# Expert weights loaded in transfers of one, two and four chunks in a float32 two-model kernel

## The chip, the core and the metric

The kernel runs on one core of one Trainium2 chip. The metric is the device time of one execution in microseconds (us); lower is better.

## The reference

One token sequence of 256 rows and 1024 features, all in float32, goes through two small models one after the other. The first has two layers. Each is a mixer (convolutions in layer 0, a gated linear recurrence in layer 1), a layer norm, and a mixture of experts: 16 experts, each with three matrices of 1024 x 1024, and every token goes to two of them. The second model has a layer of forgetting attention, a layer of dilated attention, and a convolutional feed-forward block behind each.

```
def moe(x, w_router, b_router, w1, w3, w2):
    e_idx, gates = route(xf, w_router, b_router)      # top 2 of 16
...
    def expert_block(args):
        xb, e = args
        hb = jax.nn.silu(xb @ w1[e]) * (xb @ w3[e])
        return hb @ w2[e]
```

## The kernel before

**Chunks.** All weights are read once from HBM, in the order in which they are used, in chunks of 128 partitions x 2048 float32 values: 8 KB a partition, 1 MB in all. `STREAM` (L39) lists them: 14 chunks of the first mixer, 192 of layer 0's experts (`moe0`), 14 of the second mixer, 192 of `moe1`, then those of the second model. An expert has twelve chunks: four of w1, four of w3, four of w2. Below, a chunk of a layer is named by its number 0 to 191 in `moe0` or `moe1`; expert 10 has 120 to 131.

**Places.** The chunks go to 24 places of 8 KB a partition: twelve in the tensor `ring` (places 0 to 11), five in `F` (12 to 16), four in `early` (17 to 20), and one each in `Z` (21), `XT` (22) and at another spot of `F` (23, used once a layer). Each place has its own semaphore. In the second model only seven ring places are used. `_place_stream` (L124) fixes at build time which chunk goes where. The first 24 positions of an expert layer are written out by hand (`FIRST_SLOTS`), because the places come free one by one when the mixer and the routing are done; chunk 3 is moved back to position 17 of its layer. After them each chunk takes the place whose last chunk is the oldest. Places outside the ring and Z are given out only up to position 127 of a layer, since other work needs them later. So 23 places rotate up to position 127 and 13 after it. The tables `SLOT`, `PREVIOUS` (the chunk that lay there before) and `LOADS` (how many loads a place has had) come from this.

**Loading.** `sync_load` (L327) runs on SP. For each chunk it waits until the previous chunk of its place was released, and then issues one transfer that counts on the place's semaphore. SP does this strictly in the order of the chunks, in stretches: up to chunk 119 of a layer, up to 155, and then on. The last chunk of a layer is loaded in two halves, each 4 KB a partition (L338, L339). Everything goes to one hardware queue, SP's.

**Use.** `tensor_product` (L1096) waits for a chunk with `landed` and runs it through TensorE (L1112): up to 64 tokens of the expert as the stationary operand, one pass of 512 columns of weights at a time, on the two halves of the array's columns. The profile shows eight matmul records a chunk. After its last matmul the chunk's release is signalled. Between w3 and w2 of an expert TensorE also turns the hidden values, and on alternate experts gathers the next pair's tokens (L1092) or adds the results back to the tokens (L1166). Dense weights (all but the experts') are first split into a high and a low part by ScalarE and VectorE (L360, L366) and then multiplied (L383 to L385).

**In HBM** a chunk of an expert matrix lies in one piece, its rows of 8 KB one behind the other: the array is [layer, expert, 4, 128, 2048], built by `layout`. There is also a path for experts with more than 64 tokens (`overflow_sync`, L1608), behind a branch at expert 12; it reads the same arrays.

Of the kernel before, what the change touches and what calls it, by code (L numbers as in the profile page):

```python
# [15 lines left out]
T, D, NT, KD = 256, 1024, 2, 8  # L16
# [3 lines left out]
RING, SMALL_RING, EXTRA = 12, 7, 12  # L20
PIECE, NPIECE = 512, 4
PE_TAPS = 11
CH = 2048
# [95 lines left out]
LOAD_ORDER = list(range(len(KIND)))  # L119

LAST_CHUNKS = (CHUNK["moe0"] + 191, CHUNK["moe1"] + 191)


def _place_stream():  # L124
    for layer in range(2):
        m, at = CHUNK[f"moe{layer}"], FIRST_SLOTS[layer].index(ONCE_SLOT)
        LOAD_ORDER[m + 3:m + at + 1] = LOAD_ORDER[m + 4:m + at + 1] + [m + 3]
    last, loads = [None] * (RING + EXTRA), [0] * (RING + EXTRA)
    SLOT.extend([None] * len(KIND))
    PREVIOUS.extend([None] * len(KIND))  # L130
    LOADS.extend([None] * len(KIND))
    for position, n in enumerate(LOAD_ORDER):
        slots = [*range(RING), Z_SLOT] if n < CHUNK["aq0"] else list(range(SMALL_RING))
        slot = None
        if KIND[n] == "expert":
            layer = int(n >= CHUNK["moe1"])
            i = position - CHUNK[f"moe{layer}"]
            if i < len(FIRST_SLOTS[layer]):
                slot = FIRST_SLOTS[layer][i]
            elif i < 128:  # L140
                slots += [*F_SLOTS, *SPLIT_SLOTS, XT_SLOT]
        if slot is None:
            slot = min(slots, key=lambda x: -1 if last[x] is None else last[x])
        SLOT[n], PREVIOUS[n] = slot, last[slot]
        last[slot] = n
        loads[slot] += n > 0
        LOADS[n] = loads[slot]

# [41 lines left out]
class Kernel:  # L190
    def __init__(self, nc, ctx, A, out, known):
# [9 lines left out]
        def dma_sem(name):  # L201
# [17 lines left out]
        self.X = sb("X", [128, NT, D])  # L219
        self.Z = sb("Z", [128, NT, D])  # L220
        self.XT = sb("XT", [128, KD, T])
        f_at = (nc.sbuf_base + 31) // 32 * 32
# [31 lines left out]

        self.slots = [self.ring[:, i, :] for i in range(RING)] + [
            self.F[:, 12672 - 2048 * i:14720 - 2048 * i] for i in range(5)] + [self.early[:, i, :] for i in range(4)] + [
            self.Z[:, :, :].rearrange("p h d -> p (h d)"), self.XT[:, :, :].rearrange("p k t -> p (k t)"),
            self.F[:, 2304:4352]]
        self.over = [dma_sem(f"s_over_{n}") for n in ("pe", "act", "dve", "w")]
# [18 lines left out]
    def source(self, n):  # L278
        A = self.A
# [11 lines left out]
        if name.startswith("moe"):  # L291
            return A[("w1", "w3", "w2")[i // 4 % 3]][int(name[3]), i // 12, i % 4]
        return tensors[name][order[name][i] if name in order else i]

    def chunk(self, n):
        return self.slots[SLOT[n]]

    def landed(self, n):
        return self.ring_sems[SLOT[n]], 16 * LOADS[n]

# [26 lines left out]
    def sync_load(self, first, last):  # L327
        sp = self.sp
        for n in LOAD_ORDER[first:last]:
            if n == CHUNK["aq0"] + 3:  # L330
                self.sync_rows()
            if KIND[n] == "expert" and SLOT[n] >= RING:
                sp.wait_ge(*self.extra_free(n))
            if PREVIOUS[n] is not None:
                sp.wait_ge(self.released(PREVIOUS[n]))
            src = self.source(n)
            if n in LAST_CHUNKS:
                sp.e.dma_start(self.chunk(n)[:, 0:1024], src[:, 0:1024]).then_inc(self.s_last, 16)  # L338
                sp.e.dma_start(self.chunk(n)[:, 1024:2048], src[:, 1024:2048]).then_inc(self.ring_sems[SLOT[n]], 16)  # L339
            else:  # L340
                sp.e.dma_start(self.chunk(n)[:, 0:src.shape[-1]], src).then_inc(self.ring_sems[SLOT[n]], 16)

# [1265 lines left out]
    def overflow_sync(self, layer, expert):  # L1608
        s_pe, _, _, s_w = self.over
        e, wb = self.nc.sync, self.overflow_views()["wb"]  # L1610
        for w in range(3):
            for c in range(4):
                if w + c:
                    e.wait_ge(s_pe, 4 * w + c + (1 if w == 2 else 0))
                e.dma_start(wb, self.A[("w1", "w3", "w2")[w]][layer, expert, c].rearrange("a p n -> (a p) n")
                            ).then_inc(s_w, 16)

# [851 lines left out]
    def dilated_views(self):  # L2469
        F = self.F  # L2470
        XF = self.XT[:, :, :].rearrange("p k t -> p (k t)")
        ZF = self.Z[:, :, :].rearrange("p h d -> p (h d)")
        spare = self.ring[:, 7:10, :].rearrange("p r c -> p (r c)")
# [388 lines left out]
def layout(i):  # L2862
# [34 lines left out]
    for k, n in (("w1", "moe_w1"), ("w3", "moe_w3"), ("w2", "moe_w2")):  # L2897
        w = i[n]
        a[k] = c(w.reshape(2, 16, 4, 2, 128, 1024).transpose(0, 1, 2, 4, 3, 5).reshape(2, 16, 4, 128, 2048))
    by_columns = i["moe_w2"][:, 15].reshape(2, 2, 4, 128, 2, 512).transpose(0, 4, 1, 3, 2, 5).reshape(2, 4, 128, 2048)  # L2900
    a["w2"] = c(np.concatenate([a["w2"][:, :15], by_columns[:, None]], axis=1))
# [37 lines left out]
```

## Time and profile before

| | |
|---|---|
| three runs, us | 1788.22, 1788.83, 1787.92; median 1788.22 |
| span of the profiled execution, us | 1787.6 |
| TensorE busy, share of the span | 96% |
| VectorE, ScalarE, GpSimd busy | 44%, 35%, 7% |
| read from HBM | 542.19 MB, 304 GB/s over the span |
| granted TensorE clock, mean | 0.998 |

The profiled execution has no time of its own beside its span; the span is 0.6 us below the median. The page divides the span into 40 slices of 44.7 us, and a digit is the busy share of a slice in tenths. Times in the rows below are microseconds from the start of the span unless ns is written. A busy TensorE is not a TensorE at its peak. In the rows SPq is SP's sequencer, PE is TensorE, PEld its weight loads, DVE VectorE, ACT ScalarE.

### The profile page before, as it was taken

To read this page: it belongs to the slowest core of one execution; us is meant where nothing else is said; L and a number is where in the kernel's file an instruction comes from. 1 tells how busy PE (TensorE), PEld (TensorE's weight loads), DVE (VectorE), ACT (ScalarE), POOL (GpSimd) and SP (SyncE) were. 2 spreads that over 40 slices of the span, in tenths; PEclk is the share of its full clock that TensorE was granted. 3 is DMA by queue.
4 is the path that set the end of the run, shared out by engine and by line. 5 is a ranking of instruction groups with operands and counts; after the bars stand their busy time and mean duration, and the time that the engine had idled before them with its cause. 6 is when DMAs were issued, how large, how long until landed. Compare 5 with 4: busy or idle time off the path is not lost.

```text
span 1787.6 us, 24011 instructions
## 1 busy us (share of the span) xinstructions
PE 1720.1 (96%) x10024; PEld 1114.5 (62%) x10024; DVE 790.6 (44%) x1510; ACT 624.1 (35%) x1197; POOL 121.0 (7%) x143
## 2 busy tenths in 40 slices
PE   9999999999899989999999989999999999999998
PEld 8974344433234974444333333887999899789986
DVE  6961111111003782111111011866888677768875
ACT  5541110000002661000000001666666564656664
POOL 0000000000000000000000000131111001401100
PEclk9999999999999999999999999999999999999999
DMA  9569999999999779999999999543555544435550
GB/s 390 236 249 409 423 424 423 422 422 421 419 421 419 279 298 391 423 423 424 422 422 421 419 420 420 194 141 120 188 189 177 199 159 150 141 120 179 186 189 24
DMA packets 76100, 544.91 MB, mean 305 GB/s; under 512 B 8528, under 2 KB 8528, under 8 KB 10576
## 3 DMA queue, kind: packets, MB, share of 16 engines
q1 hardware_dynamic: 75600, 542.15, 75.9%
q8 instruction: 83, 1.36, 0.3%
q10 hardware_dynamic: 384, 1.13, 0.2%
q14 instruction: 33, 0.27, 0.0%
HBM read 542.19 MB, written 1.05 MB: 304 GB/s over the span
## 4 chain that ended last, share of the span: by engine, by line
PE 71%; DMA 17%; DVE 7%; ACT 3%; issue 1%; POOL 1%; SPq 0%; DVEq 0%; ACTq 0%
PE PS L1112 25%; DMA ring<-in_w 17%; PE PS L383 12%; PE PS L385 11%; PE PS L384 11%; PE PS L1092 2%; PE PS L1166 2%; DVE wl L366 2%; PE PS L834 1%; PE PS L593 1%; ACT wh L360 1%; PE PS L1128 1%; PE PS L1180 1%; PE PS L1275 0%; DVE F L969 0%
## 5 line engine op out<-in xcount | busy, mean ns | idle before, releaser
L1112 PE MATMUL PS<-ring,F 128*64 128x512 f32 x1992 | 454.4, 597 | 30.4 <-DMA ring<-in_w 22.8
L366 DVE TENSOR_TENSOR wl<-ring,wh 128x512 fp32r<-128x512 f32 x504 | 363.6, 740 | 167.7 <-ACT wh L360 165.1
L360 ACT ACTIVATE wh<-ring 128x512 fp32r<-128x512 f32 x504 | 314.5, 631 | 273.6 <-PE PS L385 257.6
L383 PE MATMUL PS<-xh,wl 128*128 128x256 f32 x1168 | 336.5, 288 | 2.4 <-DVE wl L366 2.3
L1112 PEld LDWEIGHTS PS<-ring,F 128*64 128x64 f32 x1992 | 136.9, 137 | 322.4 <-issue 252.6
L384 PE MATMUL PS<-xl,wh 128*128 128x256 f32 x1168 | 330.4, 283 | 0.0
L385 PE MATMUL PS<-xh,wh 128*128 128x256 f32 x1168 | 330.3, 283 | 0.0
L383 PEld LDWEIGHTS PS<-xh,wl 128*128 128x128 f32 x1168 | 223.9, 192 | 5.6 <-DVE wl L366 2.7
L384 PEld LDWEIGHTS PS<-xl,wh 128*128 128x128 f32 x1168 | 223.9, 192 | 0.6
L385 PEld LDWEIGHTS PS<-xh,wh 128*128 128x128 f32 x1168 | 223.9, 192 | 0.0
L383 PE MATMUL PS<-wh,xl 128*128 128x512 f32 x352 | 142.5, 405 | 6.4 <-DVE xl L500 3.5
L385 PE MATMUL PS<-wh,xh 128*128 128x512 f32 x352 | 137.5, 391 | 0.0
L384 PE MATMUL PS<-wl,xh 128*128 128x512 f32 x352 | 137.4, 390 | 0.0
L1532 DVE COPY F<-PS 64x512 f32<-64x512 f32 x30 | 20.8, 695 | 252.2 <-PE PS L1112 252.2
L1507 DVE SCALAR_TENSOR_TENSOR F<-F,PS 128x512 f32<-128x512 f32 x32 | 22.0, 688 | 234.3 <-ACT F L1358 234.3
L1512 DVE SCALAR_TENSOR_TENSOR F<-F,PS 128x512 f32<-128x512 f32 x32 | 22.0, 688 | 201.4 <-PE PS L1112 201.4
L1112 PE MATMUL PS<-F 128*64 128x512 f32 x448 | 102.8, 594 | 0.0
L1358 ACT ACTIVATE F<-PS 128x512 f32<-128x512 f32 x32 | 19.1, 597 | 223.4 <-PE PS L1112 223.4
L1376 ACT ACTIVATE F<-PS 64x512 f32<-64x512 f32 x30 | 17.7, 592 | 217.3 <-PE PS L1112 217.3
L383 PEld LDWEIGHTS PS<-wh,xl 128*128 128x128 f32 x352 | 66.1, 188 | 27.0 <-DVE xl L500 6.4
L1366 ACT ACTIVATE F<-PS 128x512 f32<-128x512 f32 x32 | 19.0, 595 | 173.6 <-PE PS L1180 173.6
L2417 DVE SCALAR_TENSOR_TENSOR F<-PS,cols,F 128x254 f32<-128x254 f32 (+1 forms) x176 | 76.4, 475 | 1.6
(393 smaller groups left out, 1905.0 us busy)
## 6 DMA issues: line engine op xcount, KB each, us to landing
ring<-in_w SPq DMA_DIRECT2D x255, 1024.0 KB, 26.6
F<-in_w SPq DMA_DIRECT2D x56, 1024.0 KB, 23.1
ring<-in_ffn_up SPq DMA_DIRECT2D x44, 1024.0 KB, 4.9
early<-in_w SPq DMA_DIRECT2D x40, 1024.0 KB, 24.4
ring<-in_ffn_down SPq DMA_DIRECT2D x22, 1024.0 KB, 4.9
Z<-in_w SPq DMA_DIRECT2D x21, 1024.0 KB, 26.7
XT<-in_w SPq DMA_DIRECT2D x10, 1024.0 KB, 24.2
ring<-in_even_w_in SPq DMA_DIRECT2D x9, 1024.0 KB, 19.7
```

What stands on the lines that cost most here:

```text
L360: act.e.activation(self.wh[:, p % NPIECE, :], self.piece_source(p), ACT.Copy).then_inc(*self.up("w_hi", p))
L366: dve.e.tensor_tensor(self.wl[:, p % NPIECE, :], self.piece_source(p), f32(self.wh[:, p % NPIECE, :]), ALU.subtract).then_inc(*self.up("w_ ...
L383: e.matmul(out, left[1], right[0], start=first, stop=False)
L384: e.matmul(out, left[0], right[1], start=False, stop=False)
L385: return e.matmul(out, left[0], right[0], start=False, stop=last)
L1092: t = pe.e.matmul(self.PS[:, 6 + half, k4 * 128:k4 * 128 + 128], self.X[:, h, k * 128:k * 128 + 128], v["S"][:, h, :], start=(h == 0), sto ...
L1112: t = pe.e.matmul(PS[64 * half:64 * half + 64, bank, :], lhs(k), weights[:, a:a + 512], start=(k == 0), stop=(k == 7))
L1166: t = pe.e.matmul(self.PS[:, b, :], v["Gt"][:, h, d, :], v["Y"][d], start=(q == 0), stop=False)
L1507: e.scalar_tensor_tensor(out=v["hh"], in0=v["hh"], scalar=1.0, in1=PS[:, 4, :], op0=ALU.add, op1=ALU.mult).then_inc(*up("silu", layer, ex))
L1512: e.scalar_tensor_tensor(out=v["hh"], in0=v["hh"], scalar=0.5, in1=PS[:, 5, :], op0=ALU.mult, op1=ALU.mult).then_inc(*up("hidden", layer, ex))
L1532: e.tensor_copy(v["Y"][1 - o][64:128, :], PS[64:128, 5, :]).then_inc(*up("y1", layer, ex))
L2417: t = dve.e.scalar_tensor_tensor(out=dst[:, j, s:256], in0=ps[:, j, 0:256 - s], scalar=cw[:, k, 2 - s:3 - s], in1=dst[:, j, s:256], op0=AL ...
```

## The change

Expert chunks are loaded singly at positions 0 to 39 and 180 to 191 of a layer, in pairs at 40 to 63 and 152 to 179, and in groups of four, a whole expert matrix, at 64 to 151. A group goes to neighbouring places by one transfer, 16 or 32 KB a partition. `GROUPS` lists the groups of places that there are; a group of chunks takes the one whose latest chunk is the oldest, SP waits for the release of all its previous chunks, and all its chunks count as landed when the transfer has. Consumers still use and release single chunks. In HBM an expert matrix becomes [128, 8192], so that a partition's four chunks lie side by side: a single or paired load reads rows of 8 or 16 KB that lie 32 KB apart. `Z` and `XT` become the two halves of one tensor `ZX`, so that they form a pair of places.

```
--- before.py
+++ after.py
@@ -118,6 +118,23 @@
                [None] * 8 + [16, 15, None, None, 14, None, 13, None, 12, ONCE_SLOT, None, 17, 18, 19, 20, XT_SLOT])
 LOAD_ORDER = list(range(len(KIND)))
 
+
+GROUPS = {2: [(i, i + 1) for i in range(0, RING, 2)] + [(13, 12), (15, 14), (17, 18), (19, 20), (Z_SLOT, XT_SLOT)],
+          4: [(0, 1, 2, 3), (4, 5, 6, 7), (8, 9, 10, 11), (15, 14, 13, 12), (17, 18, 19, 20)]}
+FIRST_OF, SIZE = [], {}
+
+
+def _load_size(i):
+
+    if i < 40 or i >= 180:
+        return 1
+    return 4 if 64 <= i < 152 else 2
+
+
+def _oldest(groups, last):
+    return min(groups, key=lambda g: max(-1 if last[x] is None else last[x] for x in g))
+
+
 LAST_CHUNKS = (CHUNK["moe0"] + 191, CHUNK["moe1"] + 191)
 
 
@@ -126,25 +143,29 @@
         m, at = CHUNK[f"moe{layer}"], FIRST_SLOTS[layer].index(ONCE_SLOT)
         LOAD_ORDER[m + 3:m + at + 1] = LOAD_ORDER[m + 4:m + at + 1] + [m + 3]
     last, loads = [None] * (RING + EXTRA), [0] * (RING + EXTRA)
-    SLOT.extend([None] * len(KIND))
-    PREVIOUS.extend([None] * len(KIND))
-    LOADS.extend([None] * len(KIND))
+    for table in (SLOT, PREVIOUS, LOADS, FIRST_OF):
+        table.extend([None] * len(KIND))
     for position, n in enumerate(LOAD_ORDER):
-        slots = [*range(RING), Z_SLOT] if n < CHUNK["aq0"] else list(range(SMALL_RING))
-        slot = None
+        if SLOT[n] is not None:
+            continue
+        slots, size, group = [*range(RING), Z_SLOT] if n < CHUNK["aq0"] else list(range(SMALL_RING)), 1, None
         if KIND[n] == "expert":
             layer = int(n >= CHUNK["moe1"])
             i = position - CHUNK[f"moe{layer}"]
+            size = _load_size(i)
             if i < len(FIRST_SLOTS[layer]):
-                slot = FIRST_SLOTS[layer][i]
+                group = FIRST_SLOTS[layer][i] and (FIRST_SLOTS[layer][i],)
             elif i < 128:
                 slots += [*F_SLOTS, *SPLIT_SLOTS, XT_SLOT]
-        if slot is None:
-            slot = min(slots, key=lambda x: -1 if last[x] is None else last[x])
-        SLOT[n], PREVIOUS[n] = slot, last[slot]
-        last[slot] = n
-        loads[slot] += n > 0
-        LOADS[n] = loads[slot]
+        if group is None:
+            group = _oldest([g for g in GROUPS[size] if set(g) <= set(slots)] if size > 1 else [(x,) for x in slots], last)
+        SIZE[n] = size
+        loads[group[0]] += n > 0
+        for m, slot in enumerate(group, n):
+            assert LOAD_ORDER[position + m - n] == m
+            SLOT[m], PREVIOUS[m], FIRST_OF[m] = slot, last[slot], n
+            LOADS[m] = loads[group[0]]
+            last[slot] = m
 
 
 _place_stream()
@@ -217,8 +238,9 @@
         self.PS = ctx.enter_context(nc.psum_tensor("PS", [128, 8, 512], F32))
         self.cols = sb("cols", [128, NCOLS])
         self.X = sb("X", [128, NT, D])
-        self.Z = sb("Z", [128, NT, D])
-        self.XT = sb("XT", [128, KD, T])
+        self.ZX = sb("ZX", [128, 2 * CH])
+        self.Z = self.ZX[:, 0:CH].rearrange("p (h d) -> p h d", h=NT)
+        self.XT = self.ZX[:, CH:2 * CH].rearrange("p (k t) -> p k t", k=KD)
         f_at = (nc.sbuf_base + 31) // 32 * 32
         self.F = sb("F", [128, 14720])
         self.GT = self.fv(0, 8)
@@ -252,10 +274,9 @@
                                   for n, a in (("odd_gh", 13696), ("odd_gl", 14208))]
         assert nc.sbuf_base <= split_at
 
-        self.slots = [self.ring[:, i, :] for i in range(RING)] + [
-            self.F[:, 12672 - 2048 * i:14720 - 2048 * i] for i in range(5)] + [self.early[:, i, :] for i in range(4)] + [
-            self.Z[:, :, :].rearrange("p h d -> p (h d)"), self.XT[:, :, :].rearrange("p k t -> p (k t)"),
-            self.F[:, 2304:4352]]
+        ring, early = (t[:, :, :].rearrange("p r c -> p (r c)") for t in (self.ring, self.early))
+        self.places = [(ring, i * CH) for i in range(RING)] + [(self.F, 12672 - CH * i) for i in range(5)] + [
+            (early, i * CH) for i in range(4)] + [(self.ZX, 0), (self.ZX, CH), (self.F, 2304)]
         self.over = [dma_sem(f"s_over_{n}") for n in ("pe", "act", "dve", "w")]
         nums = sorted(s.num for s in self.over)
         assert nums == list(range(nums[0], nums[0] + 4))
@@ -289,14 +310,17 @@
         name = [x for x, _, _ in STREAM if CHUNK[x] <= n][-1]
         i = n - CHUNK[name]
         if name.startswith("moe"):
-            return A[("w1", "w3", "w2")[i // 4 % 3]][int(name[3]), i // 12, i % 4]
+            c = i % 4 * CH
+            return A[("w1", "w3", "w2")[i // 4 % 3]][int(name[3]), i // 12, :, c:c + SIZE[n] * CH]
         return tensors[name][order[name][i] if name in order else i]
 
-    def chunk(self, n):
-        return self.slots[SLOT[n]]
+    def chunk(self, n, size=1):
+        buffer, at = self.places[SLOT[n]]
+        return buffer[:, at:at + size * CH]
 
     def landed(self, n):
-        return self.ring_sems[SLOT[n]], 16 * LOADS[n]
+
+        return self.ring_sems[SLOT[FIRST_OF[n]]], 16 * LOADS[n]
 
     def released(self, n):
 
@@ -329,16 +353,19 @@
         for n in LOAD_ORDER[first:last]:
             if n == CHUNK["aq0"] + 3:
                 self.sync_rows()
+            if FIRST_OF[n] != n:
+                continue
             if KIND[n] == "expert" and SLOT[n] >= RING:
                 sp.wait_ge(*self.extra_free(n))
-            if PREVIOUS[n] is not None:
-                sp.wait_ge(self.released(PREVIOUS[n]))
+            for m in range(n, n + SIZE[n]):
+                if PREVIOUS[m] is not None:
+                    sp.wait_ge(self.released(PREVIOUS[m]))
             src = self.source(n)
             if n in LAST_CHUNKS:
                 sp.e.dma_start(self.chunk(n)[:, 0:1024], src[:, 0:1024]).then_inc(self.s_last, 16)
                 sp.e.dma_start(self.chunk(n)[:, 1024:2048], src[:, 1024:2048]).then_inc(self.ring_sems[SLOT[n]], 16)
             else:
-                sp.e.dma_start(self.chunk(n)[:, 0:src.shape[-1]], src).then_inc(self.ring_sems[SLOT[n]], 16)
+                sp.e.dma_start(self.chunk(n, SIZE[n])[:, 0:src.shape[-1]], src).then_inc(self.ring_sems[SLOT[n]], 16)
 
     def sync_rows(self):
 
@@ -1612,8 +1639,8 @@
             for c in range(4):
                 if w + c:
                     e.wait_ge(s_pe, 4 * w + c + (1 if w == 2 else 0))
-                e.dma_start(wb, self.A[("w1", "w3", "w2")[w]][layer, expert, c].rearrange("a p n -> (a p) n")
-                            ).then_inc(s_w, 16)
+                e.dma_start(wb, self.A[("w1", "w3", "w2")[w]][layer, expert, :, c * CH:c * CH + CH].rearrange(
+                    "a p n -> (a p) n")).then_inc(s_w, 16)
 
     def overflow_tensor(self, h, by_columns):
         s_pe, s_act, s_dve, s_w = self.over
@@ -2468,8 +2495,8 @@
 
     def dilated_views(self):
         F = self.F
-        XF = self.XT[:, :, :].rearrange("p k t -> p (k t)")
-        ZF = self.Z[:, :, :].rearrange("p h d -> p (h d)")
+        XF = self.ZX[:, CH:2 * CH]
+        ZF = self.ZX[:, 0:CH]
         spare = self.ring[:, 7:10, :].rearrange("p r c -> p (r c)")
         weights = [spare[:, i * 1152:i * 1152 + 1152] for i in range(5)] + [F[:, 10240:11392], F[:, 11392:12544], XF[:, 0:1152]]
         return dict(
@@ -2895,9 +2922,8 @@
     g = np.stack([i["odd_w_gate_a"][0], i["odd_w_gate_x"][0]])
     a["odd_gates"] = c(g.reshape(2, 4, 2, 128, 256).transpose(0, 3, 1, 2, 4).reshape(2, 128, 2048))
     for k, n in (("w1", "moe_w1"), ("w3", "moe_w3"), ("w2", "moe_w2")):
-        w = i[n]
-        a[k] = c(w.reshape(2, 16, 4, 2, 128, 1024).transpose(0, 1, 2, 4, 3, 5).reshape(2, 16, 4, 128, 2048))
-    by_columns = i["moe_w2"][:, 15].reshape(2, 2, 4, 128, 2, 512).transpose(0, 4, 1, 3, 2, 5).reshape(2, 4, 128, 2048)
+        a[k] = c(i[n].reshape(2, 16, 8, 128, 1024).transpose(0, 1, 3, 2, 4).reshape(2, 16, 128, 8192))
+    by_columns = i["moe_w2"][:, 15].reshape(2, 2, 4, 128, 2, 512).transpose(0, 3, 4, 1, 2, 5).reshape(2, 128, 8192)
     a["w2"] = c(np.concatenate([a["w2"][:, :15], by_columns[:, None]], axis=1))
     a["a_w_in"] = c(_cols(i["a_w_in_2"][0][:, :2048]))
     a["a_w_v"] = c(_blocks(i["a_w_in_2"][0][:, 2048:3072]))
```

## Rows read from the trace of the kernel before

**Rows 1.** The page: busy time, DMA per slice, chain, transfer groups
```profile
PE 1720.1 (96%) x10024; PEld 1114.5 (62%) x10024; DVE 790.6 (44%) x1510; ACT 624.1 (35%) x1197; POOL 121.0 (7%) x143
...
DMA  9569999999999779999999999543555544435550
GB/s 390 236 249 409 423 424 423 422 422 421 419 421 419 279 298 391 423 423 424 422 422 421 419 420 420 194 141 120 188 189 177 199 159 150 141 120 179 186 189 24
...
PE PS L1112 25%; DMA ring<-in_w 17%; PE PS L383 12%; PE PS L385 11%; PE PS L384 11%; PE PS L1092 2%; PE PS L1166 2%; DVE wl L366 2%; PE PS L834 1%; PE PS L593 1%; ACT wh L360 1%; PE PS L1128 1%; PE PS L1180 1%; PE PS L1275 0%; DVE F L969 0%
...
ring<-in_ffn_up SPq DMA_DIRECT2D x44, 1024.0 KB, 4.9
```

**Rows 2.** Stretches of 25 us; columns: stretch, length, busy of each engine, PEclk, DMA share, GB/s
```profile
175.00:200.00 25.00, 25.00 (x129) 10.46 (x128) 2.92 (x5) 2.27 (x4) 0.00 (x0) 1.00 1.01 424
...
425.00:450.00 25.00, 20.63 (x108) 8.75 (x106) 3.57 (x8) 2.28 (x4) 0.00 (x0) 1.00 1.01 420
450.00:475.00 25.00, 24.86 (x108) 9.00 (x106) 1.71 (x3) 1.79 (x3) 0.00 (x0) 1.00 1.01 419
```

**Rows 3.** The chain in order of time: start, us, what
```profile
153.34 20.82 PE PS L1112 x96
...
203.62 20.75 PE PS L1112 x96
...
374.31 29.28 DMA ring<-in_w
...
526.35 26.70 DMA ring<-in_w
```

**Rows 4.** TensorE's timeline, 473 to 499 us: start, us, instruction, idle before
```profile
493.37 1.94 PE L1112 MATMUL PS<-ring,F 128*64 128x512 f32 x8 [0.56 <-DMA ring<-in_w]
```

**Rows 5.** Transfers and packets, 400 to 500 us
```profile
DMA packets 5766, 42.03 MB, mean 420 GB/s; under 512 B 640, under 2 KB 640, under 8 KB 640
```

**Rows 6.** The chain in order of time, layer 1's end
```profile
1077.92 27.98 DMA ring<-in_w
```

**Rows 7.** The last half chunk of layer 1: its issue and time to landing
```profile
L339 SPq DMA_DIRECT2D ring<-in_w x1: 434/434/434, 1082.1 to 1082.1; - x1
...
DMA to landing us min/median/max: 26.3/26.3/26.3
```

**Rows 8.** One transfer into the ring and one into Z, four later: issue and landing
```profile
L341 SPq DMA_DIRECT2D ring<-in_w x1: 2104/2104/2104, 321.7 to 321.7; - x1
...
DMA to landing us min/median/max: 26.1/26.1/26.1
...
L341 SPq DMA_DIRECT2D Z<-in_w x1: 2145/2145/2145, 330.4 to 330.4; - x1
...
DMA to landing us min/median/max: 27.1/27.1/27.1
```

**Rows 9.** TensorE's timeline at chunks 49 to 55 of layer 0 and 58, 59 of layer 1
```profile
237.14 12.19 PE L1112 MATMUL PS<-ring,F 128*64 128x512 f32 x56
...
804.35 1.89 PE L1112 MATMUL PS<-F 128*64 128x512 f32 x8
```

**Rows 10.** Transfers of chunk 63, layer 0, and 71, layer 1: issue and landing
```profile
L341 SPq DMA_DIRECT2D Z<-in_w x1: 328/328/328, 219.3 to 219.3; - x1
...
DMA to landing us min/median/max: 24.2/24.2/24.2
...
L341 SPq DMA_DIRECT2D Z<-in_w x1: 327/327/327, 782.7 to 782.7; - x1
...
DMA to landing us min/median/max: 25.4/25.4/25.4
```

**Rows 11.** TensorE's timeline after an idle of 3 us, in layer 0 and in layer 1
```profile
449.78 2.79 PE L1112 MATMUL PS<-ring,F 128*64 128x512 f32 x12 [3.12 <-issue]
...
993.73 2.89 PE L1112 MATMUL PS<-ring,F 128*64 128x512 f32 x8 [3.08 <-issue]
996.35 2.74 PE L1112 MATMUL PS<-Z,F 128*64 128x512 f32 x8
```

**Rows 12.** The stretch of 3.4 us in which the granted clock was lower
```profile
994.60:998.00 3.40, 3.40 (x10) 1.21 (x8) 0.00 (x0) 0.00 (x0) 0.00 (x0) 0.50 1.03 419
```

## The prediction

> **What bounds the kernel now.** I read the page first. TensorE is busy 96% of the span, yet the chain that ended last gives 17% to one transfer line, the expert weights, and two long runs of slices show the DMA engines full at 419 to 424 GB/s [rows 1]. Those are the two expert layers, 384 chunks of 1 MB; nothing outside them is touched by this change. Next the stretches of 25 us: in layer 0 TensorE is busy all of every stretch from 175 to 375 us (the first stands for the eight), then 20.63 to 24.86 us of each 25, with the DMA engines at a share of 1.01 throughout [rows 2]. So each layer has two phases. First TensorE eats a stock of landed chunks; the stock is used up near 375 us, and from then the DMA rate sets the time. The chain in order of time says the same: from 374 to 553 us it goes from transfer to transfer [rows 3]. A chunk is eight matmul records of L1112. In its timeline a chunk that has no stock before it waits some 0.55 us for its transfer [rows 4]. Landings of 403.59 (374.31 + 29.28) and 553.05 (526.35 + 26.70) are chunks 127 and 187, last third-of-expert chunks of experts 10 and 15: 60 chunks in 149.46 us, 2.491 each [rows 3]. The last landing of a layer sets its end, and that depends on two things: time per chunk, and gaps during which no transfer is queued. TensorE's spare time is ample: it needs 25.1 us for an expert when nothing is missing (153.34 to 203.62 us is two [rows 3]), the DMA 29.9.
>
> **Part 1: fewer, longer rows.** Positions 40 to 179 of a layer, 140 chunks, go from 140 transfers to 26 pairs and 22 quads: 92 fewer. A chunk is 128 rows of 8 KB, eight rows per DMA engine, plus one small write that signals: in 100 us there are 5766 packets, 640 of them under 512 B, 16 per chunk [rows 5]. With 16 KB rows an engine has four rows per chunk, with 32 KB rows two. The trace has no row over 8 KB, but the last chunk of a layer is cut in two halves with 4 KB rows: chunk 190 lands at 1105.90 (1077.92 + 27.98) [rows 6], and the halves end at 1082.1 + 26.3 = 1108.4 [rows 7]. That is 2.5 us, against 2.49 for a whole chunk; with the rounding of these rows, eight more rows per engine cost 0 to 0.1 us. I take the middle, 0.05 us per eight rows: 0.025 saved on a chunk in a pair, 0.0375 in a quad. The ends are kept: 0 (the time goes with the bytes alone) and 0.05 and 0.075.
>
> The SP issues that go (92 a layer) are worth nothing: SP's instruction lasts 0.33 us when the queue has room [rows 10], and 2.1 us when it hasn't [rows 8], so it is the DMA engines that hold SP back, not SP them.
> A transfer alone takes 4.9 us from issue to landing [rows 1], back to back 2.49: 2.4 us of it is hidden by queued work. The Trainium skill (SBUF — State Buffer, The DMA setup-cost knee) says each transfer pays some 2 us that doesn't go with its bytes and tells one to coalesce; the trace disagrees. As a rival, from rows: if each transfer paid its 2.4 us in full, 184 fewer would save 442 us, 1346 in all. But the share is 1.01 in every full stretch [rows 2], with no room for it; I give it 0.01.
>
> **Part 2: which places.** Before, 23 places rotate up to position 127, 7 of them in F, Z or XT, and a transfer into those is quicker: chunks landing at 347.8 (321.7 + 26.1) and 357.5 (330.4 + 27.1) have four such between them, 2.43 each [rows 8]. The grouped loads use fewer of them: by the placing rule, from position 64 on 12 instead of 21 in layer 0, from 72 on 12 instead of 20 in layer 1. Each lost one costs 2.49 - 2.43 = 0.06: 0.5 us in each layer.
>
> **Part 3: a new wait.** This is the one that costs. Before, a load waits for the chunk 23 positions earlier. A group waits for the latest chunk of its places. Following the rule in layer 0: pairs run to 63, and the first quad (64 to 67) goes where 48 to 51 lie, 13 positions back. Chunk 51 is the third of the seven in the x56 row that starts at 237.14 [rows 9]; at 12.19 / 7 = 1.74 us each it is released at 242.4. Chunk 63, the last issued before it, lands at 219.3 + 24.2 = 243.5 [rows 10]. A transfer issued into an empty queue has 4.9 - 2.5 = 2.4 us before its data count, so the quad's data begin as if at 244.8 instead of 243.5: 1.3 us lost, plus whatever the pairs before it saved (0.6), which the gap swallows. The next quad needs chunk 55, released at 249.3, before this one has landed (254.6): no gap, nor later. In layer 1 the first quads find places 13 and 14 back too, and the tight one is 72 to 75, which goes where 54, 55, 58 and 59 lie. Chunk 59 is done at 806.2 (804.35 + 1.89) [rows 9], so its data begin as if at 808.6; chunk 71 landed at 782.7 + 25.4 = 808.1 [rows 10]: 0.5 us. After that the three ring quads (from position 128) suffice: a quad's work takes 7 to 11 us, two more quads are 20 us of transfer. Queued behind the waiting SP are only later loads.
>
> **Part 4: TensorE waits for whole groups.** Once the stock is gone it waits up to 3 us for a quad (9.8 us of transfer, 6.9 of work) and then works without a pause. This is the spare time it has today in pieces. After position 152 groups shrink, at 180 single chunks begin again, and the backlog (8.4 us of work at the quad of 148, falling 0.8 us with each pair) is gone by 184. So the last landing sets the end as before. Worth nothing; without the cover it costs up to the 6 us by which a quad delays its first chunks.
>
> **Sum.** Layer 0: +1.3 (gap) - 88 x 0.0375 (3.3) - 28 x 0.025 (0.7) + 0.5 = -2.2. Layer 1: +0.5 - 80 x 0.0375 (3.0) - 0.7 + 0.5 = -2.7. In all -4.9 us. The sum is made against the profiled span, 1787.6; the median of the runs, 1788.22, stands 0.6 above it. Forecast: 1788.2 - 4.9 = 1783.3. A measurement of this kernel tells 0.2%, 3.6 us, from no change.
>
> **Rivals.**
> A. Larger gain: rows cost 0.1 us per eight. Then 88 x 0.075 + 28 x 0.05 = 8.0 in layer 0 and 7.4 in layer 1, less the same 1.8 and 1.0 for gaps and places: -12.6, 1775.6. For it: the 2.43 against 2.49 of [rows 8] shows that there is overhead in the ring's places. Against it: it needs the very end of the rounding.
> B. No gain per row (the chip cuts rows again, or the cost goes with bytes). Gaps and places remain: 1.8 + 1.0 = +2.8, 1791.0, same. Nothing in the trace excludes it.
> C. Slower: reading costs more. Rows of one transfer now lie 32 KB apart, and engines that start together read at far larger strides; if memory answers 1% slower, each grouped chunk behind the gap loses 0.025: (116 + 108) x 0.025 = 5.6, with B's 2.8 in all +8.4, 1796.6. If rows bring nothing, 0.8 us more, 0.004 us a chunk, is enough to pass 0.2%. The trace shows no such stride. The Trainium skill (DMA: Bandwidth & Descriptors, Latency and other measured facts) has row pitches of large powers of two slowing copies, from 512 KiB a little, from 2 MiB a lot; no run here shows it at 32 KB.
> D. TensorE's clock. A 3.08 us idle before 993.73 [rows 11] was followed by a granted clock of 0.50 in 994.6 to 998 [rows 12], and eight records took 2.89 us instead of 1.94. An idle of 3.12 us in layer 0 was followed by no fall [rows 2, 11]. Waits of about 3 us (9.8 - 6.9) come at two of an expert's three quads, some seven times a layer; each fall loses about 1.8 us of work. Two an expert fit in the 4.8 us of spare time; three don't, by 0.6, over three or four experts: +4.2 in both layers together, 1787.5.
>
> **How the numbers follow.** Forecast case 0.43, with its own range 1780 to 1786; A 0.14; B 0.22; C 0.13; D 0.07; the setup rule 0.01. Faster by over 0.2% (under 1784.6): two thirds of the forecast case, and more at its lower side (0.32), A and the setup rule: 0.47. Slower: C, and a B in which the gaps come out larger (0.05): 0.18. Same: 0.35. The range goes from 1776 (half of A and the setup rule out) to 1792 (C out): about 0.8 inside.
>
> **What would show it.** Right: in the DMA-bound stretch 4 MB land every 9.8 us (9.96 before), packets of 32 KB; a dip of 1 to 2 us in the DMA share just after 243 us, a smaller one at 808; first waits of TensorE for a transfer come earlier, some as long as 3 us, fewer in number; the last expert landings at about 561 and 1103.5. Wrong: packets of 8 KB still (B), under 419 GB/s after 400 us (C), a clock of 0.5 in several stretches with TensorE late at position 188 (D), or dips elsewhere.

## The result, and the profile after

| | before | changed |
|---|---|---|
| median of 8 runs each, us | 1788.51 (1787.78 to 1789.19) | 1783.83 (1782.73 to 1786.35) |
| ratio | | 0.9972, 95% interval 0.9963 to 0.9982 |
| span of the profiled execution, us | 1787.6 | 1785.1 |

The change makes the kernel 4.7 us faster; 4.9 was forecast. The profiled execution of the changed kernel is its slowest run (1786.35); a second one, of the same kernel in a later series, has a span of 1782.5 and is named "the second profile" below. Line numbers move: L1112 is now L1139, L341 is L368.

The page of the changed kernel, first profile, against [rows 1]:

```profile
DMA  9669999999999779999999999433555544435550
GB/s 386 240 247 405 421 404 429 431 432 432 422 426 419 278 300 391 417 430 412 430 430 431 425 426 419 167 139 122 187 187 183 195 162 148 140 123 176 187 189 24
DMA packets 49603, 544.89 MB, mean 305 GB/s; under 512 B 5584, under 2 KB 5584, under 8 KB 7632
...
PE 71%; DMA 18%; DVE 7%; ACT 3%; issue 1%; POOL 1%; SPq 0%; DVEq 0%; ACTq 0%
...
ring<-in_w SPq DMA_DIRECT2D x32, 4096.0 KB, 29.2
ring<-in_w SPq DMA_DIRECT2D x40, 2048.0 KB, 20.9
ring<-in_w SPq DMA_DIRECT2D x66, 1024.0 KB, 10.9
```

The packets fall from 76100 to 49603, by just what the longer rows and the 184 transfers fewer make if a row of 16 or 32 KB is one packet (26496): nothing cuts it again. Where the slices read 419 to 424 GB/s before, most of the middle ones now read 429 to 432. Two slices dip, the sixth (404) and the nineteenth (412). Stretches of time show both; the kernel before first, then the changed one. Columns are the stretch, its length, busy time (and instructions) of PE, PEld, DVE, ACT and POOL, the granted clock, the DMA share and GB/s:

```profile
240.00:250.00 10.00, 10.00 (x46) 3.36 (x43) 1.31 (x3) 0.60 (x1) 0.00 (x0) 1.00 1.01 424
800.00:815.00 15.00, 15.00 (x72) 5.03 (x70) 1.91 (x6) 1.19 (x2) 0.00 (x0) 1.00 1.01 423
410.00:450.00 40.00, 34.57 (x169) 13.05 (x170) 4.26 (x9) 3.46 (x6) 0.00 (x0) 1.00 1.01 420
```
```profile
240.00:250.00 10.00, 10.00 (x48) 3.24 (x45) 1.11 (x2) 0.60 (x1) 0.00 (x0) 1.00 0.82 323
800.00:815.00 15.00, 15.00 (x74) 5.01 (x72) 2.19 (x6) 1.19 (x2) 0.00 (x0) 1.00 0.93 377
410.00:450.00 40.00, 37.59 (x182) 15.33 (x181) 4.53 (x10) 3.47 (x6) 0.00 (x0) 1.00 1.00 430
```

The DMA engines, full in before, idle for 18% of 10 us where layer 0's first quad is loaded and for 7% of 15 us at chunk 72 of layer 1. These are the two waits of part 3. The issue and the landing of chunk 63's pair (62, 63) and of the quad behind it, of one transfer each, answer to [rows 10]:

```profile
L368 SPq DMA_DIRECT2D early<-in_w x1: 328/328/328, 221.2 to 221.2; - x1
...
DMA to landing us min/median/max: 22.4/22.4/22.4
...
L368 SPq DMA_DIRECT2D ring<-in_w x1: 328/328/328, 242.8 to 242.8; - x1
...
DMA to landing us min/median/max: 12.4/12.4/12.4
```

SP issues nothing between 221.2 and 242.8, until chunk 51 is released; the pair has landed at 243.6, the quad lands at 255.2, 11.6 us later, where quads further on are 9.72 apart. So 1.9 us are lost here (2.5 in the second profile). At chunk 72 of layer 1 the quad lands 12.4 us after the one before it instead of 9.7, 2.7 us late (1.4 in the second profile).

TensorE's timeline in the DMA-bound part of layer 0 shows the new shape of the waits, against [rows 4]: a wait of some 2 us, then 32 records of a quad in one go.

```profile
431.96 7.09 PE L1139 MATMUL PS<-ring,F 128*64 128x512 f32 x32 [1.59 <-DMA ring<-in_w]
...
452.33 7.09 PE L1139 MATMUL PS<-ring,F 128*64 128x512 f32 x32 [2.06 <-DMA ring<-in_w]
...
462.30 7.09 PE L1139 MATMUL PS<-ring,F 128*64 128x512 f32 x32 [1.82 <-DMA ring<-in_w]
```

Each landing in the trace gives the time per chunk: the distance to the landing before it, divided by the chunks in the transfer. The medians over both layers, us per chunk:

| rows of | ring and early | F, Z, XT |
|---|---|---|
| 8 KB (single) | 2.492 | 2.44 |
| 16 KB (pair) | 2.451 | 2.424 |
| 32 KB (quad) | 2.430 | 2.417 |

The last landing of layer 0 moves from 563.07 to 561.19 us (561.35 in the second profile; 561 was forecast), that of layer 1 from 1108.43 to 1104.88 (1103.29; 1103.5 was forecast).

### The profile page after: what moved, and what is told of

Same layout as the page of the kernel before. It is cut to its first block, busy times and chain, and to the rows that moved or that the text cites. A ratio compares the mean times of both kernels' runs of the same rounds, so it can differ in the third digit from the quotient of the medians.

```text
span 1785.1 us, 23946 instructions
## 1 busy us (share of the span) xinstructions
PE 1715.2 (96%) x10024; PEld 1122.8 (63%) x10024; DVE 790.5 (44%) x1510; ACT 623.9 (35%) x1197; POOL 120.8 (7%) x143
## 2 busy tenths in 40 slices
DMA packets 49603, 544.89 MB, mean 305 GB/s; under 512 B 5584, under 2 KB 5584, under 8 KB 7632
## 4 chain that ended last, share of the span: by engine, by line
PE 71%; DMA 18%; DVE 7%; ACT 3%; issue 1%; POOL 1%; SPq 0%; DVEq 0%; ACTq 0%
PE PS L1139 24%; DMA ring<-in_w 14%; PE PS L410 12%; PE PS L412 11%; PE PS L411 11%; DMA early<-in_w 4%; PE PS L1193 2%; DVE wl L393 2%; PE PS L1119 1%; PE PS L861 1%; PE PS L1155 1%; PE PS L620 1%; ACT wh L387 1%; PE PS L1207 1%; PE PS L1302 0%
## 5 line engine op out<-in xcount | busy, mean ns | idle before, releaser
L1139 PE MATMUL PS<-ring,F 128*64 128x512 f32 x2144 | 478.0, 598 | 29.6 <-DMA ring<-in_w 29.1
L1139 PEld LDWEIGHTS PS<-ring,F 128*64 128x64 f32 x2144 | 152.7, 137 | 332.7 <-issue 300.1
L1139 PE MATMUL PS<-F 128*64 128x512 f32 x424 | 95.4, 593 | 1.0 <-DMA F<-in_w 1.0
L1139 PE MATMUL PS<-early,F 128*64 128x512 f32 x352 | 78.3, 594 | 4.1 <-DMA early<-in_w 4.1
```

The costliest lines, as they stand in the source:

```text
L1139: t = pe.e.matmul(PS[64 * half:64 * half + 64, bank, :], lhs(k), weights[:, a:a + 512], start=(k == 0), stop=(k == 7))
```

## The experiments

All were timed beside the kernel before on the same chip, in two series and a single run: before had medians of 1788.33 (with e1, e2, e4 and the changed kernel once more), 1789.13 (with e5 to e8) and 1789.31 (with e9). The table has them all; "per chunk" is the median for ring places, us.

| run | median, us | ratio to before (95% interval) | per chunk |
|---|---|---|---|
| changed kernel again | 1783.54 | 0.9970 (0.9958 to 0.9981) | 2.451 pair, 2.430 quad |
| e1: new arrays, single loads | 1788.36 | 0.9999 (0.9990 to 1.0008) | 2.492 |
| e2: the change's groups, 8 KB rows | 1793.93 | 1.0029 (1.0019 to 1.0039) | 2.491 pair, 2.490 quad |
| e4: quads from 56 | 1778.54 | 0.9940 (0.9926 to 0.9954) | 2.451, 2.430 |
| e5: before, places at multiples of 256 bytes | 1779.99 | 0.9951 (0.9937 to 0.9964) | 2.448, 2.442 (by layer) |
| e6: e4 and e5 together | 1775.36 | 0.9924 (0.9910 to 0.9938) | 2.424 pair, 2.417 quad |
| e7: before, 4 KB rows | 1806.53 | 1.0096 (1.0081 to 1.0112) | 2.559 |
| e8: before, places at multiples of 64 bytes | 1787.38 | 0.9989 (0.9980 to 0.9998) | 2.483 |
| e9: pairs only | 1781.04 | 0.9957 (0.9943 to 0.9971) | 2.451 |

**e1: the arrays alone.** Every chunk single, in the places of before, from the change's arrays.

```
 def _load_size(i):
-    if i < 40 or i >= 180:
-        return 1
-    return 4 if 64 <= i < 152 else 2
+    return 1
```

> The change's arrays in HBM (an expert matrix as [128, 8192]) and its joined tensor ZX, but every chunk loaded singly, with the places of before: rows of 8 KB that lie 32 KB apart. Theory rows (an 8 KB row costs some 0.01 us of an engine beyond its bytes, longer rows save it): nothing is saved or lost, within 1 us of before, chunks 2.49 us apart in the ring, packets of 8192 B. Rival stride (rows that lie apart are read slower, and the change has paid for that too): slower than before, over 2 us, chunks over 2.50 us apart. Rival layout (the new order in HBM is itself what made the change faster): 3 to 5 us faster.

The time is that of before, and a ring chunk still takes 2.492 us. Rival C's first half is out: rows of 8 KB that lie 32 KB apart are read as fast as rows side by side (the stretch from 410 to 450 us moves 420 GB/s in both). And the new order in HBM brings nothing by itself.

**e2: longer rows or fewer transfers?** The change, with its groups and places, but from the arrays of before, so that one transfer has 256 or 512 rows of 8 KB.

```
-            return A[("w1", "w3", "w2")[i // 4 % 3]][int(name[3]), i // 12, :, c:c + SIZE[n] * CH]
...
+            return w[int(name[3]), i // 12, i % 4:i % 4 + SIZE[n]].rearrange("c p n -> p c n")
...
+                if SIZE[n] > 1:
+                    to = to.rearrange("p (c n) -> p c n", n=CH)
```

> The change's transfers, groups and places as they are, but the arrays of before in HBM, so that a pair or a quad is one transfer of 8 KB rows: 256 or 512 of them. It separates longer rows from fewer transfers. Theory rows: a ring chunk takes 2.47 to 2.49 us in pairs and quads (only the signal writes are fewer), while the change's waits at chunks 64 and 72 remain; so slower than the change by 5 to 7 us and slower than before by 1 to 3. Theory transfers (the cost is per transfer, in its signal write or in the hand-over from one to the next): 2.43 us in a quad and 2.45 in a pair as in the change, and its time within 1 us.

From the page of e2 the packets, and from its stretches the one to compare with 430 GB/s in the changed kernel:

```profile
DMA packets 73155, 544.89 MB, mean 304 GB/s; under 512 B 5584, under 2 KB 5584, under 8 KB 7632
```
```profile
410.00:450.00 40.00, 38.12 (x186) 15.66 (x184) 4.59 (x10) 3.47 (x6) 0.00 (x0) 1.00 1.01 421
```

The transfers are as few as in the change (5584 small writes in both, 8528 before), yet a chunk takes 2.490 us in a transfer of 1, 2 or 4 MB. So neither the transfer nor its signal costs anything that shows when the queue is full; the row does. This run also splits the change in two: its groups and places without long rows cost 1793.93 - 1788.33 = 5.6 us, and the long rows give back 1793.93 - 1783.54 = 10.4. Both are more than was expected (1 to 3, and 5 to 7).

The 5.6 us are not the price of the two waits. With shorter rows the queue empties later, and e2's landings show 0.5 us lost at chunk 64 of layer 0 and nothing at chunk 72 of layer 1, though the DMA share falls to 0.88 and 0.97 in the two stretches. The lost places are 0.6 us, worked out from the medians of ring and F. Most of the rest are other late landings, 3.0 us more than in before's profile; they are taken up below. Likewise the 10.4 us are what long rows bring after the deeper waits that they cause: by the medians alone they save 13.2 us.

**e7: the suspected cost doubled.** The kernel before, with a chunk as two halves in HBM, so that its one transfer has 256 rows of 4 KB.

```
-        a[k] = c(w.reshape(2, 16, 4, 2, 128, 1024).transpose(0, 1, 2, 4, 3, 5).reshape(2, 16, 4, 128, 2048))
+        a[k] = c(w.reshape(2, 16, 4, 2, 128, 1024))
...
+            elif KIND[n] == "expert":
+                sp.e.dma_start(self.chunk(n).rearrange("p (h n) -> p h n", h=2), src.rearrange("h p n -> p h n")
```

> The kernel before with each expert chunk in HBM as two halves, so that its one transfer has 256 rows of 4 KB instead of 128 of 8 KB: the suspected cost doubled, same transfers, same places. Theory rows (10 ns for each row of an engine into the ring, 3 ns into F): a ring chunk takes 2.49 + 8 x 0.010 = 2.57 us, one into F 2.46, and with some 120 and 30 such chunks a layer the kernel is 18 to 23 us slower than before. If the cost of a row halves with its length, 2.49 to 2.51 and under 5 us slower.

From the page of e7 the packets, and the same stretch of it:

```profile
DMA packets 124996, 544.91 MB, mean 302 GB/s; under 512 B 8528, under 2 KB 8528, under 8 KB 108368
```
```profile
410.00:450.00 40.00, 37.19 (x176) 14.58 (x177) 4.48 (x10) 3.47 (x6) 0.00 (x0) 1.00 1.02 411
```

A ring chunk takes 2.559 us, 0.067 more for eight more rows of an engine, 8 ns each, and the kernel is 17.4 us slower, just under what was expected. Four rows fewer (the pair) save 0.041, six fewer (the quad) 0.062: 10 ns each. The cost per row is roughly the same from 4 to 32 KB.

**e4: without the dry queue.** The change, quads from chunk 56.

```
-    return 4 if 64 <= i < 152 else 2
+    return 4 if 56 <= i < 152 else 2
```

> The change with the quads from chunk 56 on instead of 64. By the placing rule a quad then finds its latest previous chunk 17 to 21 positions back from the first on, instead of 13, and SP never waits while the queue runs dry. Theory gap (the change loses 1.9 us at chunk 64 of layer 0 and up to 2.7 at chunk 72 of layer 1 to a queue that ran dry): the DMA share stays at 1.0 through 240 to 250 us and 800 to 820 us, and the kernel is 3 to 5 us faster than the change, 7 to 10 faster than before. Rival (another transfer, not the wait, made those two landings late, and it comes back elsewhere): within 1.5 us of the change.

The two stretches of e4 where the changed kernel dips:

```profile
240.00:250.00 10.00, 10.00 (x47) 3.31 (x44) 0.93 (x2) 0.60 (x1) 0.00 (x0) 1.00 0.98 423
800.00:815.00 15.00, 15.00 (x76) 5.62 (x73) 2.88 (x7) 1.19 (x2) 0.00 (x0) 1.00 0.99 428
```

These dips are gone, 323 GB/s has become 423 and 377 has become 428, and the kernel is 5.0 us faster than the changed one beside it. Only 0.3 of that can be the 16 more chunks in quads (16 x 0.021). By the landings the two waits cost the change 4.6 us in its first profile and 3.9 in the second, about as much as it brought.

The 5.0 us are not all theirs, though. In the profiles layer 0 ends 4.2 us earlier than in the change, of which the wait is 1.9 to 2.5 and the rest is late landings of the kind described below; layer 1 takes 542.3 us from last landing to last landing, against 543.7 and 541.9 in the two profiles of the change. There a smaller gap is left: chunk 64 of layer 1 finds its places 15 positions back, not the 17 or more that were expected, and its quad, issued 3.8 us before the landing ahead of it, lands 1.75 us late.

```profile
780.00:785.00 5.00, 5.00 (x26) 1.60 (x24) 0.69 (x1) 0.60 (x1) 0.00 (x0) 1.00 0.96 341
```

**e9: pairs only.**

```
-    return 4 if 64 <= i < 152 else 2
+    return 2
```

> The change with pairs where it has quads: positions 40 to 179 all in pairs. Worked from the runs so far: a ring chunk takes 2.451 us instead of 2.430 in a quad, which gives up 88 x 0.021 = 1.8 us a layer; but a pair's latest previous chunk lies 18 or more positions back, so the queue never runs dry, which gives back 1.9 to 2.5 us in layer 0 and 1.4 to 2.7 in layer 1, and more pairs use F, Z and XT (2.424). Theory gap: 1 to 3 us faster than the change, 6 to 8 faster than before. Rival (the late landings of the change are chance and not its waits): 2 to 4 us slower than the change.

It is 8.3 us faster than before, against 4.8 for the change in its series. The two ratios come from different series and their intervals overlap, so that the shorter rows win is likely and not certain; that the longer ones don't is clear. Both ends of the gap theory hold: moving the quads or dropping them takes the two dips away (e9 moves 424 and 428 GB/s in those stretches).

**The changed kernel again.**

> The changed kernel once more, on the same chip as the other three. Expected 0.2 to 0.35% faster than before, as measured. In its profile the late landings at chunk 64 (layer 0) and chunk 72 (layer 1) must come back if they are due to the wait for chunks 51 and 59; the other late landings (near chunks 72, 148 of layer 0 and 108, 174 of layer 1, 1.2 to 1.6 us each) should come at other chunks or not at all, if they are chance meetings with instruction loads. The clock falls to 0.50 once or twice a run after waits of 2.3 to 2.7 us, if rival D is right.

The late landing at chunk 64 of layer 0 is back (2.5 us), so is that at chunk 72 of layer 1, smaller (1.35). But the expectation on the others was wrong: in layer 0 they are at the same chunks in both profiles, 72, 92, 148 and 168, 0.4 to 1.5 us each, 3.5 and 2.9 us together; before had one of 1.4 from chunk 64 on. Each of them falls on an instruction load (program code for the engines), one packet on another queue that takes a DMA engine 1.0 us, as the DMA view of the stretch from 451.4 to 462.3 us of the changed kernel shows, between the landings of chunks 147 and 151 (q1 is SP's queue; packets, MB, share):

```profile
DMA packets 195, 4.48 MB, mean 411 GB/s; under 512 B 16, under 2 KB 16, under 8 KB 16
...
q1 hardware_dynamic: 193, 4.46, 95.9%
q8 instruction: 1, 0.02, 0.6%
```

In the packet records of this stretch the row that starts as the load ends also takes 1.7 us instead of 1.2, so its engine falls some 1.5 us behind. Not every instruction load makes a landing late. Counted from chunk 40 on, against the medians of each version and without the two waits, late landings add up to 8.4 to 9.4 us in the six profiles with groups (the 1.75 us of e4 among them), and to 4.0 to 7.4 in the five with single chunks. So groups seem to have this price too, some 3 us; why more landings are late with them stays open.

One part of the 2.7 us at chunk 72 in the first profile is neither: the quad lands 14.2 us after its issue there, against 12.5 in the second profile and 12.4 at chunk 64, with no instruction load in between. That also stays open.

**e5: where a row starts.** While reading the landings it stood out that F, Z and XT are quicker than the ring. The tensors' addresses in a partition offer a reason: those three begin at multiples of 256 bytes (Z at 14080, XT at 22272, F at 30464), `ring` at 131040 and `early` at 98272, each 224 bytes past a multiple of 256. One line moves both:

```
-        ring_at = (nc.sbuf_usable_end - 4 * CH * RING) // 32 * 32
+        ring_at = (nc.sbuf_usable_end - 4 * CH * RING) // 256 * 256
```

> The kernel before with ring and early moved down by 224 bytes a partition, so that their places begin at multiples of 256 bytes, as those in F, Z and XT do; before, they began 32 bytes short of a multiple of 64. Single chunks, 8 KB rows. In before an 8 KB row costs 2.49 / 8 us in a ring place and 2.44 / 8 in F. Theory alignment (the extra of the ring's rows comes from where they start): every chunk takes 2.44 us, the ring's 120 or so DMA-bound chunks a layer save 0.05 each, 12 to 14 us faster than before, more than the change brought. Rival (the extra comes from TensorE reading the ring, or from the tensor's distance from the partition's start): within 1.5 us of before, still 2.49 us.

The stretch of e5 to compare with the 420 GB/s of before:

```profile
410.00:450.00 40.00, 35.57 (x168) 13.35 (x166) 4.26 (x9) 2.87 (x5) 0.00 (x0) 0.96 1.01 427
```

A ring chunk now takes what one in F takes, 2.44 to 2.45, and the kernel before is 9.1 us faster, twice what the change brought, though less than the 12 to 14 expected (the medians make 11.3, and late landings take 1.1 more than in before's profile). The Trainium skill (DMA: Bandwidth & Descriptors, How a descriptor splits into AXI transactions) says that each transaction must start at a multiple of 256 bytes, so that a descriptor which starts off one also fetches bytes before it that cost beats. It speaks of what is read, and here it is the place written that moves. The trace agrees that there is a fixed extra for a row: 0.048 us over the eight rows of a chunk, 6 ns each, at 8 KB.

**e8: which alignment.** The same line with 64 for 256, which moves both down by 32 bytes.

> The kernel before with ring and early moved down by 32 bytes a partition, to a multiple of 64 that is none of 128 or 256. It tells which alignment counts. Theory 64 bytes: as the 256-byte version, 2.44 us a chunk, 12 to 14 us faster than before. Theory 256 bytes: 2.49 us a chunk stays, or a value between.

2.483 us instead of 2.492, and 1.8 us in the kernel's time: a multiple of 64 helps little; it takes 128 or 256, which wasn't told apart. The places start 192 bytes past a multiple of 256 here, 224 in before; whether the extra goes with that distance two points can't tell.

**e6: the version that should beat both.** e4 with e5's line.

> The change with the quads from chunk 56 (no dry queue) and with ring and early at multiples of 256 bytes: the version that should beat both. Theory alignment: quads 2.417 us a chunk and pairs 2.424 in the ring too, as in F; against the early quads alone 2 to 4 us faster, 12 to 14 faster than before. If rows and alignment are two names for one overhead, it is at most 3 us faster than the aligned kernel before. Rival: the same as the early quads alone (-9.8 us against before).

Two stretches of e6, at the first quads of layer 0 and in the middle of them:

```profile
235.00:260.00 25.00, 25.00 (x114) 8.98 (x112) 2.41 (x4) 2.38 (x4) 0.00 (x0) 1.00 1.01 435
410.00:450.00 40.00, 35.66 (x178) 14.11 (x176) 4.26 (x9) 3.21 (x6) 0.00 (x0) 1.00 1.00 431
```

1775.36 us, 13.8 less than before and the fastest of all: 2.417 us a chunk, 435 GB/s in a stretch of quads. The Trainium skill (DMA: Bandwidth & Descriptors, Where 436 GB/s comes from) gives 435.2 GB/s as the ceiling of the 16 ports; by that a chunk of 1048576 bytes takes, as an estimate, 2.409 us. The trace agrees to 0.3%, and the 0.008 us left are what two rows of 4 ns would cost; the medians of e5 and of this run differ by 4 to 5 ns for each row that an engine has more. Long rows and alignment overlap: e4 alone brings 9.8, e5 alone 9.1, both 13.8 instead of 18.9. The medians say why: alignment takes 6 to 7 ns off each row whatever its length, 0.048 us on the eight rows of a single chunk, 0.027 on the four in a pair, 0.013 on the two in a quad. They are not one thing, since longer rows still bring 4.6 us over e5 alone.

## Why the prediction was right, and where it was not

**The bound.** Right: two DMA-bound phases, the last landing sets each layer's end, nothing outside changes. e5 shows it from the other side, as it touches only the transfers.

**Part 1, rows.** Right in mechanism, mis-sized. The step took 0.05 us for eight rows of an engine, the middle of 0 to 0.1. It is 0.08 (0.041 on a chunk in a pair, predicted 0.025; 0.062 in a quad, predicted 0.0375). The true value lay inside the stated ends, and rows 6 and 7 couldn't tell more, being rounded to 0.1 us. That signals and SP's issues are worth nothing was right (e2).

**The setup rule** was rightly left at 0.01: in a full queue a transfer of 4 MB and four of 1 MB take the same time per byte (e2).

**Part 2, places.** Right in kind: by the medians 0.6 us in e2, where 1.0 was in the sum. Its reason, which the prediction didn't ask for, is the alignment (e5), and seeing that would have been worth more than the change.

**Part 3, waits.** Both places and their causes were right, issue at 242.8 for 242.4 and at 804.4 for 806.2 (layer 1 by then starts 2 us earlier), and so was the price: with the savings that a gap swallows, 1.9 us in layer 0 (1.3 + 0.6) and 1.4 in layer 1 (0.5 + 0.9). Measured are 1.9 and 2.5 at the one, 2.7 and 1.4 at the other. One reading of the rule was off without harm: in layer 1 the first quads find their places 15, 15, 13 and 15 positions back, not 13 and 14. What the part had no term for are the late landings beside instruction loads, of which groups have more.

**The sum.** The landings of the profiles add up like this, us for both layers against before. The prediction's swallowed savings stand in the first row and in the second:

| | prediction | first profile | second profile |
|---|---|---|---|
| rows and places, from chunk 40 on | -8.2 | -12.6 | -12.6 |
| the two waits | +3.3 | +4.6 | +3.9 |
| other late landings | 0 | +2.5 | +2.6 |
| before chunk 40, and between the layers | 0 | +1.9 | +1.0 |
| last landing of layer 1 | -4.9 | -3.6 | -5.1 |

The last row but one differs by as much between profiles of kernels that are alike there. So the sum came out at -4.9 for a measured -4.7 because the rows brought 4.4 us more than it had, while late landings, a term at nothing in it, took 2.5 back, and the other two rows about as much. The total owes its accuracy to luck; the mechanisms and their signs are what the runs confirm. Rival B's condition, no gain from rows, is what e2 builds: +5.6 us where B had +2.8, and again it is the late landings that make the difference.

**Part 4 and rival D.** The backlog was gone by the end of layer 0, as said. In layer 1 of the first profile it was not. The granted clock fell to 0.50 twice there. The first fall, at 908.6 us after an idle of 2.29, was covered: TensorE took 8.78 us for a quad instead of 7.09 and still had to wait for the next. At the second TensorE had waited 2.71 us, the clock fell to 0.50 for 3.4 us from 1065.6, and 16 records took 5.35 us instead of 3.65. First TensorE's timeline in the changed kernel, then the stretch around the second fall, with its mean granted clock of 0.79:

```profile
907.64 8.78 PE L1139 MATMUL PS<-ring,F 128*64 128x512 f32 x32 [2.29 <-DMA ring<-in_w]
917.40 7.09 PE L1139 MATMUL PS<-F 128*64 128x512 f32 x32 [0.97 <-DMA F<-in_w]
...
1058.82 3.65 PE L1139 MATMUL PS<-ring,F 128*64 128x512 f32 x16 [1.24 <-DMA ring<-in_w]
1065.18 5.35 PE L1139 MATMUL PS<-ring,F 128*64 128x512 f32 x16 [2.71 <-DMA ring<-in_w]
```
```profile
1062.00:1070.00 8.00, 5.29 (x20) 1.46 (x16) 0.00 (x0) 0.00 (x0) 0.00 (x0) 0.79 0.99 418
```

From there to the end of the layer TensorE waits for no transfer any more; it ends its last chunk at 1108.3, 3.4 us behind the last landing of 1104.88, where 2.4 is the usual. So a fall had a price once, 1.0 us, and in the second profile (one fall, at 915.7) none. Before had one such fall too. D as a rival is out; its mechanism, after a landing that was 1.55 us late, explains a part of why the first profile is slow.

**Rivals A, B, C.** B falls by the packet counts and e2, C by e1 and by the quads' 2.430 us. A's price per row, 0.1 us for eight, was about as near to the measured 0.08 as the forecast's 0.05, but its total wasn't, because the late landings cost what neither had.

**What the prediction could have done further.** It named the one line that costs and stopped. Following its own rule for another start of the quads would have found e4: with 56, no quad up to position 127 finds its places less than 17 positions back in layer 0, nor less than 15 in layer 1.

## What to carry to other kernels

When a queue of transfers is full, count the rows that each DMA engine moves and look at where they start: here a row cost 8 to 10 ns of its engine beyond its bytes, of which 6 went when its place began at a multiple of 256 bytes, while the number of transfers didn't matter. Grouping loads also groups their waits: before making transfers larger, work out for each how many positions back the chunk lies for whose release it waits, since a queue that runs dry at the seam between two sizes can take back a third of what the longer rows give. Try the smaller change first; one line of alignment did more than the new loader.

## What the runs showed of the hardware that was not expected

- 1 MB in 128 rows of 8 KB takes 2.492 us into a place 32 bytes off a multiple of 64, 2.483 at a multiple of 64, and 2.44 to 2.45 at a multiple of 256.
- What alignment saves is 6 to 7 ns a row at 8, 16 and 32 KB alike.
- A transfer of 4 MB in rows of 8 KB is no faster per MB (2.490) than four of 1 MB (2.492).
- Rows 32 KB apart in HBM are read at the same 420 GB/s as rows side by side.
- Rows of 32 KB go as one packet each, and reach 435 GB/s into aligned places.
- An instruction load of one packet, 1.0 us of one engine, can delay the landing of a transfer by up to 1.5 us, at the same chunks in two executions.
